# Sixteen slots of the FFN's first product as seven block products each

## The reference

```python
h = rmsnorm(x, norm_ffn_pre[l])
gate, up = jnp.split(h @ w_ffn_in[l], 2, axis=-1)      # (512, 1024) @ (1024, 2*2816)
x = x + rmsnorm((jax.nn.silu(gate) * up) @ w_ffn_out[l], norm_ffn_post[l])
```

## Time and profile before

| | |
|---|---|
| time, median of 3 runs | 965.72 us (963.72 to 965.87) |
| profiled execution, its own time | 963.78 us |
| its span, first to last instruction | 962.1 us |
| TensorE busy, share of the span | 951.5 us, 99% |
| GpSimd, DVE, ScalarE busy | 433.6, 520.1, 379.5 us |
| TensorE's granted clock | full throughout |
| FFN's first product | 592.7 to 836.6 us |

### The profile page before, as it was taken

How to read it: one execution, slowest core, us unless ns; L and a number is a source line. 1 busy time by engine, 2 the same in 40 slices (tenths; PEclk the granted TensorE clock), 3 DMA queues, 4 the chain that set the end, 5 groups by cost and what they waited for, 6 DMA issues and landing times.

```text
span 962.1 us, 15030 instructions
## 1 busy us (share of the span) xinstructions
PE 951.5 (99%) x6138; PEld 771.1 (80%) x6138; DVE 520.1 (54%) x721; ACT 379.5 (39%) x510; POOL 433.6 (45%) x349
## 2 busy tenths in 40 slices
PE   9999999999999999999999999999999999999997
PEld 7887877787787778777778888888888888888886
DVE  5877876856576756888667738622322223311115
ACT  6424516533551562346653426422332223322232
POOL 4874424433272254343045653454445444565552
PEclk9999999999999999999999999999999999999999
DMA  8333222332333274238154653243433333222312
GB/s 272 124 99 120 101 98 89 132 131 69 131 132 110 74 251 136 90 104 290 67 197 171 245 175 88 56 119 97 118 90 87 87 105 113 88 87 90 120 54 87
DMA packets 107910, 117.74 MB, mean 122 GB/s; under 512 B 2896, under 2 KB 86864, under 8 KB 107856
## 3 DMA queue, kind: packets, MB, share of 16 engines
q1 hardware_dynamic: 100512, 102.80, 33.2%
q10 hardware_dynamic: 7344, 14.16, 3.8%
HBM read 100.70 MB, written 16.25 MB: 122 GB/s over the span
## 4 chain that ended last, share of the span: by engine, by line
PE 37%; issue 37%; POOL 22%; DVE 1%; ACT 0%; DMA 0%; POOLq 0%; SPq 0%; DVEq 0%; ACTq 0%
POOL w_lo L600 22%; PE ps L1631 12%; PE ps L1632 12%; PE ps L1633 12%; DVE x_ct L1161 1%; DVE rstd_x L1084 0%; DMA w_raw<-w_in 0%; DVE proj L1091 0%; ACT w_hi L697 0%; POOL wide_mask L647 0%; POOLq L661 0%; PE ps L1705 0%; POOL head_rows L673 0%; POOL head_rows L671 0%; DVE b_lo L1065 0%
## 5 line engine op out<-in xcount | busy, mean ns | idle before, releaser
L600 POOL TENSOR_TENSOR w_lo<-w_raw,w_hi 128x512 fp32r<-128x512 f32 x296 | 412.5, 1424 | 493.6 <-ACT w_hi L697 493.2
L697 ACT CAST w_hi<-w_raw 128x2048 fp32r<-128x2048 f32 x74 | 141.1, 1907 | 137.5 <-PE ps L1633 115.7
L1746 PE MATMUL ps<-a_hi,w_hi 128*128 128x512 f32 x384 | 155.9, 406 | 1.0 <-ACT spill_buf L783 0.9
L1631 PE MATMUL ps<-a_hi,w_hi 128*128 128x512 f32 (+1 forms) x400 | 152.8, 382 | 0.1
L1746 PE MATMUL ps<-a_lo,w_hi 128*128 128x512 f32 x384 | 152.6, 397 | 0.0
L1632 PE MATMUL ps<-a_lo,w_hi 128*128 128x512 f32 (+1 forms) x400 | 152.3, 381 | 0.0
L1633 PE MATMUL ps<-a_hi,w_lo 128*128 128x512 f32 (+1 forms) x400 | 152.2, 381 | 0.0
L1746 PE MATMUL ps<-a_hi,w_lo 128*128 128x512 f32 x384 | 151.3, 394 | 0.0
L1576 DVE TENSOR_TENSOR f_gate<-ps,g_up 128x512 f32<-128x512 f32 x22 | 15.2, 691 | 156.3 <-PE ps L1633 156.1
L1631 PEld LDWEIGHTS ps<-a_hi,w_hi 128*128 128x128 f32 x400 | 75.2, 188 | 15.4 <-POOL w_lo L600 0.8
L1746 PEld LDWEIGHTS ps<-a_hi,w_hi 128*128 128x128 f32 x384 | 72.1, 188 | 19.2 <-issue 1.7
(11 more groups left out here) (328 smaller groups left out, 1492.2 us busy)
## 6 DMA issues: line engine op xcount, KB each, us to landing
w_raw<-w_in SPq DMA_DIRECT2D x32, 1024.0 KB, 5.1
w_raw<-w_ffn_in SPq DMA_DIRECT2D x44, 512.0 KB, 4.6
spill<-spill_buf ACTq DMA_DIRECT2D x27, 512.0 KB, 3.2
w_raw<-w_ffn_out SPq DMA_DIRECT2D x11, 1024.0 KB, 5.0
w_raw<-w_branch SPq DMA_DIRECT2D x5, 1024.0 KB, 8.0
g_ab<-spill SPq DMA_DIRECT2D x8, 512.0 KB, 5.0
w_raw<-w_out SPq DMA_DIRECT2D x4, 1024.0 KB, 7.3
proj<-spill SPq DMA_DIRECT2D x1, 3072.0 KB, 15.0
```

The lines of the kernel that those rows point to most:

```text
L600: g.tensor_tensor(w_lo[:, b, c], w_raw[:, b, c], w_hi[:, b, c].bitcast(F), ALU.subtract).then_inc(lo_ready, 1)
L697: s.copy(w_hi[:, b], w_raw[:, b]).then_inc(hi_ready, 1)
L1631: t_.matmul(dst, w0, a0, start=first, stop=False)
L1746: last = t_.matmul(ps[:, 6 + half], w[:, kt, half * P:(half + 1) * P], a, start=(kt == 0 and step == 0), stop=(kt == KT - 1 and step == 2))
```

## The change

Six slots (`N_PLAIN`) stay as they are, apart from being written out without a loop. The other 16 (`N_MIX`) are each a product of a 2x2 block matrix by a 2x2 block matrix, done in seven block products instead of eight (the Winograd form of Strassen's algorithm). The activation is cut into tokens 0 to 255 and 256 to 511 (`EARLY`, `LATE`) and channels 0 to 511 and 512 to 1023; the weights of a slot into gate and up, and the same halves of channels. A block product is 4 channel tiles x 3 matmuls, 256 tokens wide.

The seven forms of the activation (three blocks as they are, four sums and differences) are made once, during the plain slots: DVE rebuilds the activation as `a_norm` = `a_hi` + `a_lo`, scales it by `row_scale`, and makes the four mixed forms; ScalarE makes the high half `form_hi` and writes the negated cast to `form_lo`; and a DMA that GpSimd issues adds the form itself to `form_lo` in SBUF, which leaves the low half. The sums of weight blocks are made per slot: on DVE `t12` (two), `t3` in place in `w_raw`, `t4`. Their high halves come from ScalarE. The low halves come from GpSimd (`b_low`, `t12_low`, 128x1024 each), from DVE (`t4_low`), and, for the two blocks in `late_lo`, from an accumulating DMA again (`late_low`); the first from DVE (`first_late_low`). The seven products accumulate in three half banks per slot, `x_ps`, `y_ps` and `c11_ps`, with copies and differences between them: `keep_p1` and `keep_q5` on ScalarE, `less_u2` and `up_of_2` on DVE. Sigmoids and gating are done for each token half by itself.

A raw buffer is loaded again (`mix_raw_free`) when `b_low`, `t4` and the accumulating DMA that reads it are done. New semaphores are mostly earlier ones used on. `late_hi`, `late_lo` and the small tiles lie in the memory of `a_hi` and `a_lo`, `f_hi` and `f_lo` in that of forms that are no longer read. The load of `gain_ffn` moves behind the last block product.

```diff
@@ SyncE @@
+            for s in range(N_MIX):
+                if s < 2:
+                    sp.wait_ge(lo_ready, lo_of(S_FOUT + s - 2))
+                else:
+                    mix_raw_free(s - 2)
...
@@ GpSimd @@
+            def late_low(s):
+                pool.wait_ge(late_neg_made.sem, late_neg_made.base + s)
+                pool.dma_start(late_lo[:, s % 2, 0:2 * BLK], w_raw[:, mix_buf(s), 2 * BLK:],
+                               accum_op=ALU.add).then_inc(late_lo_landed[s % 2].sem, 16)
...
+            low(S_FIN + 1, (S_FIN + 1) % 2)
+            low(S_FIN + 2, (S_FIN + 2) % 2)
+            form_low(A11)
+            low(S_FIN + 3, (S_FIN + 3) % 2)
+            form_low(A12)
+            form_low(A22)
+            low(S_FIN + 4, (S_FIN + 4) % 2)
+            form_low(S1)
...
+            low(S_FIN + 5, (S_FIN + 5) % 2)
+            b_low(0)
+            t12_low(0)
+            b_low(1)
+            t12_low(1)
+            late_low(1)
+            for n in range(N_MIX - 2):
+                b_low(n + 2)
+                t12_low(n + 2)
+                late_low(n + 2)
...
@@ ScalarE @@
+            plain_sigmoid(0)
+            plain_high(2)
+            form_high(A11)
+            plain_sigmoid(1)
...
+            b_high(0)
+            t12_high(0)
+            b_high(1)
+            plain_sigmoid(5)
+            keep_p1(0)
...
+            for n in range(N_MIX):
+                if n > 0:
+                    sigmoid_1(n)
+                if n == 0:
+                    keep_p1(1)
+                if n + 2 < N_MIX:
+                    b_high(n + 2)
+                if 0 < n < N_MIX - 1:
+                    keep_p1(n + 1)
+                if n + 2 < N_MIX:
+                    t12_high(n + 2)
...
+                if n > 0:
+                    sigmoid_2(n - 1)
+                if n + 1 < N_MIX:
+                    t4_high(n + 1)
+                    keep_q5(n + 1)
+                if n + 2 < N_MIX:
+                    late_high(n + 2)
...
@@ DVE, ahead of row_scale @@
+            dve.wait_ge(h_lo_ready, 2 * NT)
+            for j in range(KT // 2):
+                k = slice(2 * j, 2 * j + 2)
+                last = v.tensor_tensor(a_norm[:, k], a_hi[:, k].bitcast(F), a_lo[:, k].bitcast(F), ALU.add)
+            link(last)
             dve.wait_ge(rows_spread, 1)
             link(v.tensor_copy(row_scale[:], ps[:, 4]))
...
+            plain_act(0)
+            norm(0)
+            norm(1)
+            plain_act(1)
+            norm(2)
+            norm(3)
+            mixed_forms()
...
+            t12(1)
+            t3(1)
+            t4(1)
+            plain_act(5)
+            first_late_low()
...
+            for n in range(1, N_MIX):
+                gate_of_1(n)
+                less_u2(n)
+                if n + 2 < N_MIX:
+                    t12(n + 2)
+                    t3(n + 2)
+                act_2(n - 1)
+                if n + 1 < N_MIX:
+                    t4_low(n + 1)
+                if n + 2 < N_MIX:
+                    t4(n + 2)
+                act_1(n)
+                up_of_2(n)
...
@@ TensorE @@
+            def block_product(dst, hi, lo, at, f, first):
+                for k in range(KT // 2):
+                    c = slice(at + k * P, at + (k + 1) * P)
+                    t_.matmul(dst, hi[:, c], form_hi[f][:, k], start=first and k == 0, stop=False, skip_group_check=not first)
+                    t_.matmul(dst, hi[:, c], form_lo[f][:, k], start=False, stop=False, skip_group_check=not first)
+                    last = t_.matmul(dst, lo[:, c], form_hi[f][:, k], start=False, stop=k == KT // 2 - 1, skip_group_check=not first)
+                return last
...
+            p1(0)
+            q5(0)
+            c11(0)
+            for s in range(N_MIX - 1):
+                u2(s)
+                p1(s + 1)
+                if s > 0:
+                    c21(s - 1)
+                q5(s + 1)
+                c12(s)
+                u3(s)
+                c11(s + 1)
```

More of the change, by code:

```diff
@@ L239, in hybrid_layer @@
         f_all, o = arena("f_all", [P, FT, SEQ], 0)
[L240 to L248, removed]
+        BLK, HALF = KT // 2 * P, SEQ // 2
@@ new lines, in hybrid_layer @@
+        row, _ = arena("row", [P, D], row_at)
+        gain_ffn, _ = arena("gain_ffn", [P, D], AT_FORM(A22))
+        f_hi, f_lo = [], []
+        for i in range(2):
+            t, o = arena(f"f_hi_{i}", [P, 2, SEQ], AT_FORM(i), R)
+            f_hi.append(t)
+            t, o = arena(f"f_lo_{i}", [P, 2, SEQ], o, R)
+            f_lo.append(t)
+        a_norm, _ = arena("a_norm", [P, KT, SEQ], 4 * SEQ * 6)
+        s_raw, _ = arena("s_raw", [P, 4, KT // 2, HALF], 4 * SEQ * 14)
+        f_gate = nc.alloc_sbuf_tensor_at("f_gate", [P, SEQ], F, offset=AT_RUN)
@@ L1596, in _ @@
-            f_low(0)
-            f_low(1)
-            ffn_in(N_FIN // 2 - 1)
-            ch.end(N_FIN // 2)
+            plain_act(0)
[5 more added lines that the diff above has]
+            mixed_forms()
+            plain_act(2)
+            plain_act(3)
+            dve.wait_ge(lo_group_landed[group_of(S1)], 16)
+            t12(0)
+            t3(0)
+            dve.wait_ge(lo_group_landed[group_of(RS)], 16 * len(lo_groups[group_of(RS)]))
@@ new lines, in _ @@
+            t4(0)
+            plain_act(4)
+            t12(1)
[3 more added lines that the diff above has]
+            first_late_low()
+            gate_of_1(0)
+            less_u2(0)
+            t4_low(0)
+            t12(2)
+            t3(2)
+            act_1(0)
+            up_of_2(0)
+            t4(2)
+            t4_low(1)
+            for n in range(1, N_MIX):
[11 more added lines that the diff above has]
+                up_of_2(n)
+                if n + 2 >= N_MIX:
+                    f_low(n + 2 - N_MIX)
@@ L1600, in _ @@
+            act_2(N_MIX - 1)
             for m in range(2, N_FOUT):
@@ L2142, in _ @@
+            for m in range(1, N_FOUT - 2):
                 pe.wait_ge(f_lo_ready, m + 1)
-                for i, t in enumerate((2, 3, 1 - last_pair, last_pair) if m == 0 else range(NT)):
-                    if m == 0 and t == last_pair:
-                        pe.wait_ge(f_read, N_FIN)
-                    last = ffn_out(m, t, i > 0)
+                for t in range(NT):
+                    last = ffn_out(m, t, t > 0)
                 last.then_inc(slot_used, 1)
@@ L2164, in _ @@
                     for k in range(2):
[L2165 removed]
+                        last = three(ps[:, 2 * t + half], f_hi[m % 2][:, k, s_], f_lo[m % 2][:, k, s_], wh[:, k, c], wl[:, k, c],
                                      False, m == N_FOUT - 1 and k == 1)
```

422 lines of the change are left out of this document (366 added, 56 removed).

## The result

| | before | after |
|---|---|---|
| median of four runs, us | 964.72 (963.68 to 965.87) | 972.68 (972.19 to 973.74) |
| ratio, 95% interval | | 1.0087 [1.0072, 1.0102] |
| profiled execution's own time (span), us | 963.8 (962.1) | 972.19 (970.5) |
| mean granted clock | | 0.989 |

Slower by 0.87%; 971 was forecast. A time that follows "waits" is TensorE's: the distance between two matmul starts, less the 0.227 or 0.120 us that one takes there at full clock.

The account below looks back on a forecast made before the run. TensorE was taken to bound the kernel (busy 951.5 of 962.1 us). Terms -13.1 + 2.2 + 2.1 + 1.8 + 3.7 + 4.0 + 5.7 + 0.5 = +6.9 on 963.8 gave 970.7, stated as 971; range 956 to 989.

Parts of the forecast that it names:

- The saving: TensorE's mixed slots: seven block products take 10.06 us against 10.88, 13.1 us saved in 16 slots.
- Slot 2: Way in: a_norm adds delay w_lo (+2.2), and norm(0), norm(1) alternate with GpSimd's w_lo pieces (+2.1).
- Slot 5, +1.8: Way in: t12(0), t3(0), t4(0) on DVE alternate with GpSimd's w_lo pieces of slot 5, +1.8 us.
- c11(0): Way in: c11(0) waits for keep_p1(0), behind plain_sigmoid(5), plain_act(5) and DVE's turn 1 sums, +3.7 us.
- c21(1), +4.0: Way in: late_low(1) starts late, so load(3) and up_of_2(1) are late and c21(1) waits, +4 us with hand-overs.
- X = 6: Accumulating DMA's assumed time from issue to landing, 6 us with its issue on GpSimd, between bounds 3.2 and 15.0.
- The turns, +5.7: Steady mixed slots: 10.5 us each instead of 10.06, from the fourth on, 13 x 0.44 = +5.7 us.
- The ring of transfers: Raw buffer's reload waits for the accumulating DMA; a turn of 15.3 or 12.3 us plus its landing must fit 20.12.
- the end: Last slots: f_low(0) stands behind a full DVE, +0.5 us.
- Rival A: Faster: DMA lands within 4.8 us, only slot 2 and c11(0) stall; 958.7 us (954 to 962), chance 0.25.
- Rival B: Slower by more: accumulating DMA takes 8 us or more; 976 at 8, 989 at 10; chance 0.23.
- Rival C: No change: full way-in loss (13.8, end 0.5), no steady loss; 965.0 us, chance 0.12.

Follow-up runs that it names:

- experiment 4: The kernel after with DVE's four a_norm adds moved from ahead of row_scale to behind plain_act(0): 975.93 us, ratio 1.0121.
- forms_dve: The kernel after with all seven forms' low halves subtracted on DVE, without GpSimd's accumulating DMAs and ScalarE's negated copies: 966.86 us, ratio 1.0032.
- split_forms: The kernel after with four mixed forms' low halves on DVE, half-length GpSimd pieces, b_high(0), t12_high(0), keep_p1(0) ahead of ScalarE's sigmoids: 962.14 us, ratio 0.9976.
- Experiment 1: The run forms_dve: the kernel after with all seven forms' low halves subtracted on DVE instead of made by accumulating DMAs: 966.86 us.
- Experiment 6: forms_dve with keep_p1(0) ahead of plain_sigmoid(5) on ScalarE: 966.37 us, ratio 1.0025.
- Experiment 5: The kernel after with 12 extra matmuls before p1(0) and 9 before c11(0), inside TensorE's waits: 972.43 us, ratio 1.0076.
- t12_high_first: split_forms with t12_high(1) ahead of plain_sigmoid(5) on ScalarE: 967.24 us, ratio 1.0035.
- experiment 3: The kernel after with GpSimd's b_low and t12_low each in two 128x512 pieces instead of one of 128x1024: 971.07 us, ratio 1.0075.
- forms_dve_b_first: split_forms with all seven forms' low halves subtracted on DVE: 963.70 us, ratio 0.9996.
- adds_later: The run of experiment 4: the kernel after with the a_norm adds behind plain_act(0) on DVE: 975.93 us, ratio 1.0121.

## Why the prediction was right, and where its working was not

**The saving: right.** Half-wide matmuls come 120 ns apart, and a slot of seven products takes 10.08 us where 10.06 was reckoned: -12.8 for -13.1. (The 13 ns that the prediction puts on one half-wide matmul are those of two: 120 is 6.5 over half of 227. Its 8.7 us are reckoned with 6.5.)

**Slot 2: right in size, in part by luck, 4.2 for 4.3.** The adds ahead of `row_scale` hold up `w_lo` (2.4 more than before), shown by experiment 4, whose move took it away. The norms' share was foreseen as turns with the pieces; the rows have only 0.7 of that, for 2.1, and 1.3 of matmuls at the lower clock behind the first wait, which was not forecast.

**Slot 5, +1.8: did not occur.** `t12(0)` ran at 665.64, when slot 5's pieces were long made. But the late load is not what spared the slot. In forms_dve and split_forms the load was on time and DVE's subtractions took turns with these pieces, which lasted 8.4 and 9.0 us for the four instead of 5.0; slot 5 waited for none of them, since GpSimd was far enough ahead. The term was mis-sized.

**`p1(0)`: not in the sum, and the largest wait, 6.5.** The prediction priced one accumulating DMA and asked what it does to its own reader. It did not ask what four of them in a row do to the load that SyncE issues 0.1 us later. Nor did it ask when DVE, which waits for these DMAs before `t4(0)`, could go on. Experiment 1 shows the burst as the cause: without it 5.3 us come back and the loads land in 5.1; how the 6.5 divide between the load and DVE's own wait is an estimate only (2.8 and the rest). "Hidden behind 10.88 us of matmuls" was said of ScalarE's casts for the forms and never of their DMAs.

**`c11(0)`: right, 3.5 for 3.7,** through the chain named. Experiment 6 adds what the prediction missed: taken away by itself, with the load on time, it brought 0.7, no more than the noise, because `plain_act(5)` and `t12_low(1)` are as late.

**The clock, +4.4: not in the sum.** In the gaps of 6.5 and 3.5 the granted clock fell, and the matmuls after them took 0.21 where 0.12 was reckoned. Experiment 5 took 3.7 of that out of the rows and gained 1.1: as a term of the sum it stands for time that other waits would largely have taken.

**`c21(1)`, +4.0: missed, 0.8.** It was laid out from X = 6 and an undisturbed way in. In the versions run it lay between 0.5 and 2.0 (none in t12_high_first, behind a wait of 7.5), also where `p1(0)` did not wait at all (0.7 in split_forms), so the size was wrong, not hidden by the other stalls. The accumulate's 4.7 for 6 is worth 1.3 of it at most; the rest of the layout was not taken apart.

**The turns, +5.7: mis-sized, +1.7, and by another wait.** The ring of transfers was the step: X = 6 gave 10.65 or 10.06, and I took 10.5 for 13 turns; nine turns came at 10.26 and the others at 10.08. At X = 4.7 the ring fits into two slots, and in the steady part neither DVE's `t12` nor ScalarE's `b_high` is released by a load (the row at 760.07, and its neighbours, name none). What is left is the other half of the step, `up_of_2` behind GpSimd's pieces at SBUF, with 0.2 a turn; experiment 3 takes it all away by halving the pieces, and in experiment 4 whole pieces leave TensorE no wait either. The Trainium skill ("SBUF — State Buffer", section "Who interferes with whom") has the rule: a VectorE instruction with two SBUF inputs and a GpSimd instruction that reads SBUF exclude each other for a whole instruction. The traces agree: DVE's 128x512 operations on two SBUF operands take 2.77 us beside whole pieces and 1.79 beside half ones, and 0.68 where an operand is in PSUM.

**The sum.** Forecast -13.1 + 20.0, measured -13.1 + 21.1. Of the 20.0, 8.0 were right in place and near in size (7.7, of which 1.3 by the clock). The remaining 12.0 (slot 5, `c21(1)`, the turns, the end) measured 2.5 (0.8 and 1.7), 9.5 less; in their place stand 10.9 that were not forecast, `p1(0)` and the clock. That the total is right is luck: two errors of opposite sign are nearly of one size.

**Rival A** (958.7) had the ring right: the DMA lands within 4.8 us and the steady part costs 1.7 us. It failed on the way in, where it allowed 8.0 and 19.4 came. split_forms comes within 3.4 us of its time. **Rival B**, a slow accumulate in steady state, is excluded by 4.7. **Rival C** was right in kind: the saving is real in every turn and spent before the first one.

**What stays open:** how the 6.5 at `p1(0)` divide between the load and DVE's wait for the DMAs; where the 1.6 us between split_forms and forms_dve_b_first lie, whose waits differ by half a microsecond at most; why DVE's turns with whole pieces vary in adds_later; and whether slot 2's 3.3 us and the 3.9 before `q5(1)` can both go; each order tried gave one back elsewhere.

## What to carry to other kernels

A change that saves a little in each of many steps pays for its beginning: lay out the way in for every engine and every queue, and add up the bytes of all DMAs that are in flight together, not the latency of each. If a wait hangs on an engine whose list has no gap, another order of that list mostly moves the wait. What shortened the sum here was to let the engines behind it (ScalarE, with `b_high(0)` and `keep_p1(0)`) do first what does not need it, together with shorter pieces on GpSimd (3.5 us), and to take work off the list (1.6). And a total that comes out right says nothing of its terms: check each against its own row.

## What the runs showed of the hardware

- An accumulating DMA inside SBUF, 512 KB, lands 4.7 us after its issue in the mixed slots (15 of them) and 11.8 when four are issued in 3.65 us beside loads (medians). By the page's queues, q0 (these) takes 6.5% of the engines' span for 11.54 MB, q1 33.2% for 102.80 MB: 1.7 times as much engine time for a byte.
- With four of them in flight beside the loads, the DMA engines were busy 0.97 of the 12 us from 656 at 219 GB/s, where loads alone reach 345, and a 512 KB load takes 9.8 us instead of 4.7 (medians of four); the worst of them, issued 0.49 us after the first accumulating DMA, took 17.3. In t12_high_first, beside one accumulating DMA, such a half took 9.3.
- Each costs GpSimd itself 0.87 us at its issue, during which no piece runs.
- After TensorE's idle 6.5 us, with a second idle stretch of 3.5 behind it, the granted clock was 0.72, 0.55 and 0.60 in the stretches from 668 to 688; where matmuls of no use filled both, it was 1.00.
- Two half-length pieces of GpSimd cost 3.0 to 3.5 us where the whole one took 2.4 to 2.9, and the kernel's steady turns are still shorter with them than in the kernel after (10.08 for 10.26): DVE is shut out for less at a time.
